# Late projection of tiles 4 to 8 in 352-column products from one weight buffer instead of 176-column products from two

## The reference, cut to what matters

```python
xn = rms_norm(x, norm1_g)
qr, kr, vr, gr, qs, ks, vs = split(xn @ w_in)        # w_in is 1024 x 2816, float32
# retention over chunks of 128 tokens, sliding-window attention, output projection w_out
h = x + concat(retention, attention) @ w_out
q = (rms_norm(h) @ peer_w_q)                         # 8 heads, two halves
# per token and head: top 16 of 128 keys in each half, top 16 of the 256 sums
h1 = einsum('thkd,td->thk', peer_u[idx], xt)         # idx: 128 experts per token
a = gelu(h1) * gates
y = final_norm(h + einsum('thk,thkd->td', a, peer_v[idx]))
```

## Time and profile before

| what | value |
| --- | --- |
| median of 3 runs | 2974.87 us (2971.45 to 2983.48) |
| profiled execution, its own time | 2974.4 us |
| span of the profile | 2972.6 us |
| busy: TensorE, VectorE, ScalarE, GpSimd | 76%, 70%, 37%, 41% of the span |
| moved by DMA | 1214.41 MB, mean 409 GB/s |
| of it by the fetches' queue | 1082.20 MB |

### The profile page before, as it was taken

One profiled execution on the slowest core, in us unless ns is written; L12 is line 12 of the kernel. 1 busy time (PEld: TensorE's weight loads), 2 busy tenths in 40 slices (PEclk: granted clock), 3 DMA queues, 4 the chain that ended last, 5 costly groups with the idle time before them and its releaser, 6 DMA issues.

```text
span 2972.6 us, 33489 instructions
## 1 busy us (share of the span) xinstructions
PE 2270.6 (76%) x10572; PEld 1130.7 (38%) x10572; DVE 2077.3 (70%) x5291; ACT 1094.6 (37%) x3330; POOL 1211.2 (41%) x1069
## 2 busy tenths in 40 slices
PE   8898887577799577996876776866776668769665
PEld 6666534122466224672343232512242123315211
DVE  3685558965786656865568865797579765996965
ACT  2233433343343432443334343333434353342322
POOL 0133344444433343333443444444444444444443
PEclk9999989778999788997898678977898789987866
DMA  9999999999999999999999999999999999999998
GB/s 365 382 418 415 381 421 420 413 409 421 420 397 386 423 420 412 406 415 419 421 421 392 420 416 421 420 395 421 421 421 417 413 412 421 419 405 361 409 414 356
DMA packets 197043, 1214.41 MB, mean 409 GB/s; under 512 B 28320, under 2 KB 47592, under 8 KB 63104
## 3 DMA queue, kind: packets, MB, share of 16 engines
q0 software_dynamic: 148608, 1082.20, 88.5%
q1 hardware_dynamic: 48256, 130.07, 11.1%
HBM read 1192.48 MB, written 20.23 MB: 408 GB/s over the span
## 4 chain that ended last, share of the span: by engine, by line
DMA 35%; DVE 28%; PE 24%; issue 5%; ACT 5%; POOL 3%; SPq 1%; DVEq 0%; POOLq 0%; ACTq 0%
DMA ring<-in_peer_uv,idxg 29%; DVE ring L1946 14%; PE ps L1097 12%; PE ps L751 6%; POOL ring L657 3%; DVE columns L1779 3%; DVE columns L1773 2%; PE ps L1050 2%; ACT ring L1158 2%; DMA wo<-in_xT_sample 1%; DMA wo<-in_w_in 1%; DVE columns L1785 1%; DVE columns L1849 1%; DVE columns L1852 1%; PE ps L1000 1%
## 5 line engine op out<-in xcount | busy, mean ns | idle before, releaser
L657 POOL DMA_INDIRECT ring<-in_peer_uv,idxg x1024 | 1189.3, 1161 | 1608.6 <-PE ps L1097 1421.2
L1097 PE MATMUL ps<-ring 128*64 128x512 f32 x4096 | 1242.6, 738 | 636.2 <-ACT ring L1158 635.1
L1946 DVE SCALAR_TENSOR_TENSOR ring<-ring,xlo 128x1024 f32<-128x1024 f32 x512 | 627.5, 1226 | 356.9 <-DMA ring<-in_peer_uv,idxg 318.7
L1946 DVE SCALAR_TENSOR_TENSOR ring<-ring,xhi 128x1024 f32<-128x1024 f32 x512 | 627.4, 1225 | 322.0 <-DMA ring<-in_peer_uv,idxg 306.7
L1097 PEld LDWEIGHTS ps<-ring 128*64 128x64 f32 x4096 | 288.5, 158 | 1346.3 <-ACT ring L1158 924.8
L1405 ACT ACTIVATE small<-small 128x2 f32<-128x2 f32 x512 | 103.8, 203 | 1498.6 <-DVE ring L1946 1497.5
L1050 PEld LDWEIGHTS ps<-work,wq 128*128 128x128 f32 x2304 | 276.9, 198 | 85.5 <-issue 84.2
L1158 ACT ACTIVATE ring<-gdiag,small 128x64 f32<-128x64 f32 x1024 | 300.3, 340 | 16.8
L1050 PE MATMUL ps<-work,wq 128*128 128x128 f32 (+1 forms) x2304 | 295.8, 282 | 1.1 <-ACT work L1158 1.1
L1158 ACT ACTIVATE gdiag<-fold,gateg 128x64 f32<-128x64 f32 x1024 | 292.9, 333 | 3.1
L751 PE MATMUL ps<-wo 128*128 128x176 f32 x1680 | 274.7, 321 | 10.4 <-DMA wo<-in_w_in 10.4
(11 more groups left out here) (214 smaller groups left out, 1594.1 us busy)
## 6 DMA issues: line engine op xcount, KB each, us to landing
wo<-in_w_in SPq DMA_DIRECT2D x41, 704.0 KB, 11.5
ring<-in_peer_uv,idxg POOLq DMA_INDIRECT x1024, 11.9
wo<-in_w_out SPq DMA_DIRECT2D x4, 4096.0 KB, 17.2
ring<-in_w_in SPq DMA_DIRECT2D x8, 1408.0 KB, 8.5
wq<-in_w_q SPq DMA_DIRECT2D x4, 2048.0 KB, 25.2
proj_scratch<-wo SPq DMA_DIRECT2D x93, 88.0 KB, 8.8
columns<-proj_scratch SPq DMA_DIRECT2D x7, 896.0 KB, 11.0
h<-in_x_prompt SPq DMA_DIRECT2D x9, 512.0 KB, 8.5
```

The lines of the kernel that those rows point to most:

```text
L657: nc.gpsimd.indirect_dma_start(row[r], None, A["peer_uv"], bass.IndirectOffsetOnAxis(ap=experts, axis=0)).then_inc(ld_row[r], 16)
L1097: mm = nc.tensor.matmul(acc[side * HP:(side + 1) * HP, n * 512:(n + 1) * 512], row_u[r][:, 0:HP], row_v[r][:, n * 512:(n + 1) * 512], star ...
L1946: ins = stt(row_u[r], row_u[r], 1.0, (xlo, xhi)[unit % 2][:], ALU.mult, ALU.mult, accum_out=dot[:, r:r + 1])
```

## The change

The 16 chunks for tiles 4 to 8 become 8 pairs of chunks. One load brings two chunks (1408 KB), one product has 352 columns (the two chunks side by side in the moving operand), one copy and one store move 352 columns (176 KB). The two weight buffers become one of twice the size, so a pair's load is issued after the last product of the pair before it. Staging has two buffers of 352 columns in place of six of 176. A gap keeps its 40 ticks: a pair every 11 ticks, its tiles at +0, +2, +4 and +6 ticks, the sample tile right behind the fourth.

```diff
-LATE_TILES = [(1,)] * LCH + [(2, 3)] * LCH + [(4, 5, 6, 7, NB)] * LCH
+LATE_TILES = [(1,)] * LCH + [(2, 3)] * LCH + [(4, 5, 6, 7, NB)] * (LCH // 2)
...
-HALFWAY = LAST_OF[2 * LCH + LCH // 2 - 1] + 1
+PAIR_CHUNKS = LCH // 4
+HALFWAY = LAST_OF[2 * LCH + PAIR_CHUNKS - 1] + 1
...
-GAP_SLOTS = 4 * LCH // 2
-GAP_FROM, GAP_TICKS = 94, 40
+GAP_FROM, PAIR_TICKS = 94, 11
...
-    chunk, tile = divmod(at, 5)
-    return front_at(gap + 2) + GAP_FROM + (chunk * 4 + min(tile, 3)) * GAP_TICKS // GAP_SLOTS
+    pair, tile = divmod(at, 5)
+    return front_at(gap + 2) + GAP_FROM + pair * PAIR_TICKS + 2 * min(tile, 3)
...
-        stg_late = [part(LW) for _ in range(5)] + stg_wide
-        w_late = [part(KC * LW) for _ in range(2)]
+        stg_late = [part(2 * LW) for _ in range(2)]
+        w_late = part(2 * KC * LW)
...
-            return w_late[l % 2], ld_last[l % 2], (l - 2 * LCH) // 2 + 1
+            return w_late, ld_last, l - 2 * LCH + 1
...
-            return (ps[:, q % 2, 0:LW] if q < AHEAD else F[4 + q % 2][:, 0:LW])
+            if q < AHEAD:
+                return ps[:, q % 2, 0:LW]
+            return F[4 + q % 2][:, 0:LW if q < EARLY else 2 * LW]
...
-            return (stg_early if q < EARLY else stg_late)[q % STG]
+            return stg_early[q % STG] if q < EARLY else stg_late[(q - EARLY) % 2]
+
+        def stage_free(q):
+
+            if q < EARLY:
+                return st_pj[q % STG], 16 * (q // STG)
+            return st_pj[(q - EARLY) % 2], 16 * (EARLY // STG + (q - EARLY) // 2)
...
-                elif l >= 2 * LCH and l % (LCH // 2) >= 2:
-                    sp.wait_ge(pj_mm, NCH + LAST_OF[l - 2] + 1)
+                elif l % PAIR_CHUNKS:
+                    sp.wait_ge(pj_mm, NCH + LAST_OF[l - 1] + 1)
                 buf, landed, _ = late_w(l)
-                sp.dma_start(buf, A["w_in"][l % LCH]).then_inc(landed, 16)
+                if l < 2 * LCH:
+                    sp.dma_start(buf, A["w_in"][l % LCH]).then_inc(landed, 16)
+                    return
+                at_ = 2 * (l - 2 * LCH)
+                sp.dma_start(buf.rearrange("p (l f) -> p l f", l=2), A["w_in"][at_:at_ + 2].rearrange("l p f -> p l f")
+                             ).then_inc(landed, 16)
...
-                sp.dma_start(rows_d[:, c * LW:(c + 1) * LW], late_stage(q)).then_inc(st_pj[q % STG], 16)
+                wide = LW if q < EARLY else 2 * LW
+                sp.dma_start(rows_d[:, c * wide:(c + 1) * wide], late_stage(q)).then_inc(stage_free(q)[0], 16)
...
-                    for l in range(l0, l0 + LCH // 2):
-                        if l > l0 + 1:
-                            yield late_tick(LAST_OF[l - 2]) + 4
+                    for l in range(l0, l0 + PAIR_CHUNKS):
+                        if l > l0:
+                            yield late_tick(LAST_OF[l - 1]) + 2
                         load_late(l)
...
-                o, w = late_bank(q), by_k(buf)
+                halves = 1 if q < EARLY else 2
+                o = late_bank(q).rearrange("p (a n) -> p a n", a=halves)
+                w = buf.rearrange("p (a k n) -> p k a n", a=halves, k=KC)
...
-                        mm = nc.tensor.matmul(o, tokens_T(n, k), w[:, k, :], start=(k == 0), stop=(k == KC - 1))
+                        mm = nc.tensor.matmul(o, tokens_T(n, k), w[:, k], start=(k == 0), stop=(k == KC - 1))
...
-                    act.wait_ge(st_pj[q % STG], 16 * (q // STG))
+                    act.wait_ge(*stage_free(q))
```

More of the change, by code:

```diff
@@ L54 @@
 LW = D_IN // LCH
-LATE_TILES = [(1,)] * LCH + [(2, 3)] * LCH + [(4, 5, 6, 7, NB)] * LCH
+LATE_TILES = [(1,)] * LCH + [(2, 3)] * LCH + [(4, 5, 6, 7, NB)] * (LCH // 2)
 PIECES = [(l, l % LCH, n) for l, tiles in enumerate(LATE_TILES) for n in tiles]
-FIRST_OF = {l: min(q for q, piece in enumerate(PIECES) if piece[0] == l) for l in range(3 * LCH)}
-LAST_OF = {l: max(q for q, piece in enumerate(PIECES) if piece[0] == l) for l in range(3 * LCH)}
+FIRST_OF = {l: min(q for q, piece in enumerate(PIECES) if piece[0] == l) for l in range(len(LATE_TILES))}
+LAST_OF = {l: max(q for q, piece in enumerate(PIECES) if piece[0] == l) for l in range(len(LATE_TILES))}
 FIRST_TILE = LAST_OF[LCH - 1] + 1
@@ L331, in build @@
         ld_late = [sem(f"ld_late{i}") for i in range(3)]
-        ld_last = [sem(f"ld_last{i}") for i in range(2)]
+        ld_last = sem("ld_last")
         ld_lower, ld_upper = sem("ld_lower"), sem("ld_upper")
@@ L431, in store_late @@
                 sp.wait_ge(pj_out, NCH + q + 1)
-                sp.dma_start(rows_d[:, c * LW:(c + 1) * LW], late_stage(q)).then_inc(st_pj[q % STG], 16)
+                wide = LW if q < EARLY else 2 * LW
+                sp.dma_start(rows_d[:, c * wide:(c + 1) * wide], late_stage(q)).then_inc(stage_free(q)[0], 16)
             def late_stored(count):
+                if count > EARLY:
+                    for q in range(count - 2, count):
+                        of, before = stage_free(q)
+                        sp.wait_ge(of, before + 16)
+                    return
                 for i in range(STG):
@@ L443, in late_loads @@
                 for part_ in range(2):
-                    l0 = 2 * LCH + part_ * LCH // 2
+                    l0 = 2 * LCH + part_ * PAIR_CHUNKS
                     yield front_at(part_ + 2) + PICK_AT + 12
@@ L747, in project_late @@
                         group = k % 4
-                        mm = nc.tensor.matmul(o[group * SPAD:(group + 1) * SPAD, :], of_sample(xT_late, k), w[:, k, :],
+                        mm = nc.tensor.matmul(o[group * SPAD:(group + 1) * SPAD], of_sample(xT_late, k), w[:, k],
                                               start=(k < 4), stop=(k >= 4), skip_group_check=True)
                     else:
-                        mm = nc.tensor.matmul(o, tokens_T(n, k), w[:, k, :], start=(k == 0), stop=(k == KC - 1))
+                        mm = nc.tensor.matmul(o, tokens_T(n, k), w[:, k], start=(k == 0), stop=(k == KC - 1))
                 mm.then_inc(pj_mm, 1)
```

## The result

The changed kernel takes 2999.72 us in the median of 6 runs (2996.45 to 3006.91), the kernel before on the same chip 2972.86 (2966.82 to 2983.48). The ratio is 1.0097, with an interval of 1.0079 to 1.0114: **slower by 27 us**, 0.97%. The prediction said slower, 3017 us in a range of 2984 to 3056. So 5.7 us of the difference between the two traces belong to the executions and not to the change.

What follows compares the result with a forecast made beforehand. It took the DMA to bound the kernel and TensorE's queue the two gaps; 216.2 us of work, 69.6 of waits and 15.0 of slow starts made 300.8 against 257.75, so 2974.4 + 43 = 3017 us, range 2984 to 3056.

Steps and rivals of the forecast that it cites:

- The DMA bounds the kernel, TensorE the gaps, and what a gap grows by the kernel grows by: Whole kernel at about 421 GB/s; in both gaps TensorE's queue is the bound, and their growth adds fully to the total.
- TensorE's work shrinks by almost nothing: In the gaps, 64 narrow pieces become 32 wide ones, 3.5 us less; sample pieces taken at 1.46 us.
- The loads: Three exposed loads a gap, each landing in 11.5 us; 11.6 us from sample product to next product, 69.6 in all.
- of 6 to 8 us six times: Sign: first wide piece of pairs 2, 3 and 4 in each gap waits this long for `in_w_in`.
- The clock: After each of six waits in the gaps TensorE restarts slowly, 2.5 us a stall, 15.0 us in all.
- The sum: Both gaps: 216.2 us plus 69.6 of waits and 15.0 of slow starts, 300.8 against 257.75, so +43 us.
- Quick landing: Rival: gap loads land in 6.6 us as at the quiet start; -1.3 us, 2973 us; chance 0.10.
- The rule of the Trainium skill: About 2.0 us fixed plus bytes over 436 GB/s, 5.3 us for a gap load; kernel at 2965 us.
- The DMA-bound case: Rival: add_pair calls between pairs wait for fetches, gaps shrink to 243.7 us; -14, 2960 us; chance 0.05.
- The staging case: Rival: in the gaps stores land late (18.7 us), so copies and products wait; +19 on the sum, 3036 us; chance 0.07.

Runs made afterwards that it cites:

- The filled gaps: Kernel before with eight dummy wide products added three times in each gap: 2992.38 us, ratio 1.0052.
- one narrow buffer: Kernel before with one weight buffer of 704 KB loads in place of two, narrow pieces and spread order kept: 3070.81 us, ratio 1.0320.
- the filled ordinary stretches: Kernel before with the same 48 dummy wide products placed in ordinary stretches of blocks 5 and 6: 2973.93 us, ratio 0.9996.
- the bunched order: Changed kernel with a pair's tiles at +0, +0, +2, +2 ticks: 3029.18 us; with the third tile's store also ahead of the next load: 2996.15 us.
- two buffers: Changed kernel with tiles 5 to 7 projected from tile 4's tokens and a second wide weight buffer: 2962.83 us, against 2991.15 us without that buffer.
- the second trace: Changed kernel measured again without alteration, on the chip of three later runs: 3004.91 us, ratio 1.0102.

## Why the prediction was right, point by point

- **The DMA bounds the kernel, TensorE the gaps, and what a gap grows by the kernel grows by.** Held. The filled gaps cost +18.9 us for +19.8 of gap, one narrow buffer +97.3 for +97.4, the filled ordinary stretches nothing that shows. It holds for gaps of the same order of work; the bunched order lost time that its gaps' length didn't show.
- **TensorE's work shrinks by almost nothing.** Held. A wide piece took 4.93 us start to start (851.17 to 856.11) against 4.87 forecast, the sample 1.32 against 1.46. Even with two buffers wide pieces bring some 3 us at most.
- **The loads.** The mechanism held: where the block boundary did not lie over them, they are on the chain whole, five of six. The landing time was mis-sized a little: 11.6 us from sample product to next product was forecast six times, 69.6 in all; the trace has 9.41, 11.84, 11.17, 9.92, 10.37 and 11.23, together 63.9. The landing itself, forecast at 11.5 us, was 10.3 in the mean. Idle times "of 6 to 8 us six times" were 5.76, 5.34, 7.52, 3.87 and 7.58, so five times and from 3.9 up; the sixth fell into the block boundary, where other waiting stood already.
- **The clock.** 2.5 us a stall were taken, 15.0. The six first pieces took 6.37, 7.77, 7.92, 4.93, 7.92 and 7.96 us start to start, that is 1.4, 2.8, 3.0, nothing, 3.0 and 3.0 over 4.93: 13.3. Keeping TensorE busy in the waits bought 7 us of the kernel, 8 to 12 of the gaps. It shortened the slow starts; that they account for the whole 7 us is not shown.
- **The sum.** 300.8 us for both gaps, 294.1 in the trace: 5.7 less in the waits, 1.7 less in slow starts, 0.7 more in everything else. Outside, where nothing was to move, 3.9 us were regained, and the profiled execution lay 5.7 us higher against its median than that before. 43.1 - 6.7 - 3.9 - 5.7 = 26.8, measured 26.9. So of the 16 us by which the forecast was too high, 6.7 were its own terms. Part of those 5.7 us may lie in the gaps themselves: in the second trace they took 290.0 us.
- **The rivals.** Quick landing did not occur in this kernel (8.8 to 11.7 us). The rule of the Trainium skill ("DMA: Bandwidth & Descriptors", section "Anatomy of one DMA"), from which 5.3 us a load were worked out as an estimate, is given there for transfers issued by GpSimd, while these loads are SyncE's. No run here shows it for them: the nearest were 5.9 us at the quiet start and 6.2 us in the bunched order, where fetches were held back. The DMA-bound case did not occur: 363 and 352 GB/s. The staging case did not occur in the changed kernel's gaps, but in two others that ran closer together or issued the store late (16.6 and 29.6 us of waits in the first gap). Its condition, that a store is issued as soon as its copy is done, was missing from the prediction.

What stays open: what the 3.9 us outside the gaps are; and how much of the 3 to 4 us of idle TensorE that each gap has with two wide buffers comes of the waits for stores. No version tried was faster than the kernel before with all of the computation done.

## What to carry to other kernels

Merging two buffers that take turns into one of double size keeps the bytes and nearly all of TensorE's time and gives the overlap away: ask first what work lies between the issue of each load and its use, and price the load by its landing beside the real traffic. Where moving work for more cover is tried, look at what else that work releases (here the ring) and at what stands behind the waiting issue in its queue. And before any estimate, find out whether the stretch is bound by the engine that will wait: 29 us of extra work cost 19 in one place and nothing in another.

## What was not expected of the hardware

- The landing time of one and the same 1408 KB load differed with what ran beside it: 6.2 to 8.5 us in the bunched orders, where fetches were held back, 8.8 to 11.7 in the changed kernel, and 12.0 to 12.2 and 10.7 to 10.9 in the two gaps with two wide buffers, beside 398 and 393 GB/s. 704 KB landed in 6.3 to 8.8 us with one narrow buffer, against medians of 14.6 and 11.0 before, where more was under way. This fits a load that hastens itself a little by stopping the traffic around it, but no run changes that alone.
- Idle time of TensorE of 3.87 us and more ahead of a wide piece was always followed by a slow one, 6.5 to 8.0 us instead of 5.00. Shorter idle times went either way: 2.05, 2.43 and 3.48 us were followed by 5.00 us, but 2.45 by 6.69, 3.15 by 6.69 and 2.13 by the following, from the second trace of the changed kernel:

```profile
906.13 6.64 PE L772 MATMUL ps<-wo 128*128 128x352 f32 x16 [2.13 <-DMA wo<-in_w_in]
```

  So no length of idle time can be named from these traces up to which a wait leaves the clock alone. Dummy products on resident operands in five of the waits kept the pieces behind them at 4.90 to 5.00 us in all but one case, the 3.15 us above (granted clock 1.00 and 0.98 over the two gaps, against 0.92 and 0.93 in the changed kernel).
